# A two-layer hybrid decoder step on one core: opening with later slot requests, products of ones, and squares added pairwise

## The reference, cut to what matters

```python
def rmsnorm(x, gain):
    y = xf * lax.rsqrt(jnp.mean(xf * xf, axis=-1, keepdims=True) + RMS_EPS)
    return (y * gain.astype(jnp.float32)).astype(x.dtype)
...
def swiglu(x, w_gate, w_up, w_down):
    return (jax.nn.silu(x @ w_gate) * (x @ w_up)) @ w_down
...
    x = x + 0.5 * swiglu(rmsnorm(x, ffn1_norm), ffn1_w_gate, ffn1_w_up, ffn1_w_down)
```

## Time and profile before

| | us |
|---|---|
| median of 3 runs | 1161.32 (1161.1 to 1161.77) |
| profiled execution, its time | 1161.36 |
| its span, first to last instruction | 1159.3 |
| TensorE busy in the span | 1148.5 |
| GpSimd, VectorE, ScalarE busy | 806.0, 598.5, 532.8 |
| DMA | 180.91 MB, mean 156 GB/s |

### The profile page before, as it was taken

One profiled execution on the slowest core, in us unless ns is written; L12 is line 12 of the kernel. 1 busy time (PEld: TensorE's weight loads), 2 busy tenths in 40 slices (PEclk: granted clock), 3 DMA queues, 4 the chain that ended last, 5 costly groups with the idle time before them and its releaser, 6 DMA issues.

```text
span 1159.3 us, 22766 instructions
## 1 busy us (share of the span) xinstructions
PE 1148.5 (99%) x7914; PEld 1132.1 (98%) x7914; DVE 598.5 (52%) x878; ACT 532.8 (46%) x801; POOL 806.0 (70%) x421
## 2 busy tenths in 40 slices
PE   7999999999999999999999999999999999999999
PEld 6999999999899999999999999999998999999998
DVE  5865562239967544432258655522598764444100
ACT  5444444444765444444444444444457654444332
POOL 6776667777776766667667766677786776666674
DMA  8444445557535544445565444455573654443453
GB/s 295 153 162 146 145 118 149 149 171 221 159 120 165 173 146 154 143 122 148 159 196 161 147 146 146 119 149 162 179 211 114 183 154 153 152 152 124 138 149 107
DMA packets 72203, 180.91 MB, mean 156 GB/s; under 512 B 10210, under 2 KB 25826, under 8 KB 72162
## 3 DMA queue, kind: packets, MB, share of 16 engines
q1 hardware_dynamic: 71680, 179.23, 49.8%
q10 hardware_dynamic: 482, 1.16, 0.3%
HBM read 176.78 MB, written 3.58 MB: 156 GB/s over the span
## 4 chain that ended last, share of the span: by engine, by line
PE 96%; DMA 1%; DVE 1%; ACT 1%; POOL 0%; issue 0%; SPq 0%; DVEq 0%
PE bank L611 28%; PE bank L614 28%; PE bank L612 28%; PE bank L897 2%; PE bank L899 2%; PE bank L898 2%; PE bank L671 1%; PE bank L672 1%; PE bank L670 1%; DMA x<-in_xT 1%; DMA raw<-in_w 0%; PE bank L879 0%; PE bank L857 0%; PE bank L732 0%; PE bank L839 0%; POOL w_lo L506 0%
## 5 line engine op out<-in xcount | busy, mean ns | idle before, releaser
L506 POOL TENSOR_TENSOR w_lo<-raw,w_hi 128x1024 fp32r<-128x1024 f32 (+2 forms) x351 | 766.5, 2189 | 321.0 <-ACT w_hi L985 320.5
L985 ACT ACTIVATE w_hi<-raw 128x1024 fp32r<-128x1024 f32 (+2 forms) x351 | 336.5, 961 | 439.2 <-PE bank L614 423.2
L611 PE MATMUL bank<-xg_hi,w_hi 128*128 128x320 f32 x1552 | 481.8, 310 | 0.9 <-DVE tmp L1264 0.9
L614 PE MATMUL bank<-xg_hi,w_lo 128*128 128x320 f32 x1552 | 479.6, 309 | 0.0
L612 PE MATMUL bank<-xg_lo,w_hi 128*128 128x320 f32 x1552 | 479.5, 309 | 0.0
L611 PEld LDWEIGHTS bank<-xg_hi,w_hi 128*128 128x128 f32 x1552 | 291.3, 188 | 3.7 <-issue 1.9
L612 PEld LDWEIGHTS bank<-xg_lo,w_hi 128*128 128x128 f32 x1552 | 291.4, 188 | 0.4
L614 PEld LDWEIGHTS bank<-xg_hi,w_lo 128*128 128x128 f32 x1552 | 291.3, 188 | 0.0
L611 PE MATMUL bank<-h_hi,w_hi 128*128 128x320 f32 x704 | 217.5, 309 | 0.0
L612 PE MATMUL bank<-h_lo,w_hi 128*128 128x320 f32 x704 | 217.5, 309 | 0.0
L614 PE MATMUL bank<-h_hi,w_lo 128*128 128x320 f32 x704 | 217.5, 309 | 0.0
(11 more groups left out here) (188 smaller groups left out, 816.6 us busy)
## 6 DMA issues: line engine op xcount, KB each, us to landing
raw<-in_w SPq DMA_DIRECT2D x223, 512.0 KB, 3.8
raw<-in_w SPq DMA_DIRECT2D x64, 384.0 KB, 3.0
raw<-in_w SPq DMA_DIRECT2D x64, 320.0 KB, 2.9
k_all<-in_cache_kT SPq DMA_DIRECT2D x32, 128.0 KB, 3.5
v_past<-in_cache_v SPq DMA_DIRECT2D x32, 128.0 KB, 2.8
cst<-in_consts ACTq DMA_DIRECT2D x1, 997.0 KB
out_yT<-x SPq DMA_DIRECT2D x1, 960.0 KB, 4.9
x<-in_xT SPq DMA_DIRECT2D x2, 320.0 KB, 3.8
```

What stands on the lines that cost most here:

```text
L506: pool.tensor_tensor(w_lo[:, j, 0:count * P], raw[:, j, 0:count * P], w_hi[:, j, 0:count * P].bitcast(F32), ALU.subtract).then_inc(split.s ...
L611: pe.matmul(out, hi, in_hi[:, k, :], start=first and n == 0, stop=False)
L614: mm = pe.matmul(out, lo, in_hi[:, k, :], start=False, stop=last and end)
L985: act.activation(w_hi[:, j, 0:count * P], raw[:, j, 0:count * P], ACT.Copy).then_inc(split_hi.sem, 1)
```

## The change

Six edits, all in the opening of layer 0, and one in the order of layer 0's first step:

1. SyncE waits for piece 1 of the input before it requests slots (0,1) to (0,3). It then requests slot (1,0), ahead of `load_small`; the three other slots of iteration 1 follow behind it, and the loop starts at iteration 2.
2. The matrix of ones is filled first, with a semaphore of its own. TensorE multiplies ones with ones (128 columns, float32, into bank 7, never read) twelve times before its first real product, and once behind each of the eight high x high products of column 0.
3. The squares of tiles 0 to 3 move from ScalarE to VectorE, right behind the low parts of their piece. Tiles 4 and 5 are ScalarE's, behind its rounding of slot (0,1); 6 and 7 are VectorE's.
4. The `tensor_reduce` over eight squares becomes four additions: tiles 0, 1 + 2, 3; 4, 5 + 6, 7; the two results (640 elements each); and the last pair into `sumsq` (320). Each waits for the one before it.
5. TensorE's `sum_squares` stands behind column 1 instead of column 2.
6. In `first_step` of layer 0 the root comes before the rounding of slots (1,0) and (1,1), as in layer 1.

```diff
+WARM_PRODUCTS = 12
...
             load_x(2)
+            sp.wait_ge(x_in[1].sem, 16)
             for j in range(1, 4):
                 load_slot(0, BASE_G1, 0, j, w8, W8_G1, HALVES8)
+            load_slot(0, BASE_G1, 1, 0, w8, W8_G1 + 1, HALVES8)
             for L in range(DEPTH):
                 load_small(L)
-                with sp.Fori(1, IT_G) as i:
+                for j in range(0 if L else 1, 4):
+                    load_slot(L, BASE_G1, 1, j, w8, L * W8_ROWS + W8_G1 + 1, HALVES8)
+                with sp.Fori(2, IT_G) as i:
                     load(L, BASE_G1, i, w8, L * W8_ROWS + W8_G1 + i, HALVES8)
...
+            def idle_products(count):
+
+                for _ in range(count):
+                    pe.matmul(bank[7][:, 0:P], ones[:, :], ones[:, :], start=True, stop=True)
+
...
                     pe.matmul(bank[j][:, 0:TOK], w_hi[:, j, k * P:(k + 1) * P], xg_hi[:, k, :], start=k == 0, stop=False)
+                    if j == 0:
+                        idle_products(1)
...
                     if j == 0:
+                        pe.wait_ge(ones_ok.sem, 1)
+                        idle_products(WARM_PRODUCTS)
                         first_part(j, range(0, 4), half_hi.sem, 1, half_lo.sem, 1)
...
-                    if j == 2:
+                    if j == 1:
                         sum_squares(0, 0)
...
-                if L:
-                    root_of_norm(L, 0)
+                root_of_norm(L, 0)
                 round_slot(L, BASE_G1, 1, 0, HALVES8)
                 round_slot(L, BASE_G1, 1, 1, HALVES8)
-                if L == 0:
-                    root_of_norm(L, 0)
...
             round_first(1, raw_in[0].sem)
-            for d in range(DT // 2 - 2):
+            round_piece(2)
+            round_slot(0, BASE_G1, 0, 1, HALVES8)
+            for d in range(4, 6):
                 square_first(d)
-            round_piece(2)
-            for d in range(DT // 2 - 2, DT // 2):
-                square_first(d)
-            for j in range(1, 4):
+            for j in range(2, 4):
                 round_slot(0, BASE_G1, 0, j, HALVES8)
...
+            dve.memset(ones[:, :], 1.0).then_inc(ones_ok.sem, 1)
...
+            def squares_too(d):
+                dve.tensor_tensor(tmp[:, d, :], x[:, d, :], x[:, d, :], ALU.mult).then_inc(squared_too.sem, 1)
+
+            def add_squares(out, a, b, count):
+                dve.wait_ge(squared_too.sem, count)
+                return dve.tensor_tensor(out, a, b, ALU.add)
+
             for n, piece in enumerate(X_PIECES):
                 dve.wait_ge(x_in[n].sem, 16)
                 for d in range(*piece):
                     input_rest(d, d, d)
-            for d in range(DT // 2, DT):
-                dve.tensor_tensor(tmp[:, d, :], x[:, d, :], x[:, d, :], ALU.mult).then_inc(squared_too.sem, 1)
-            dve.wait_ge(squared_first.sem, DT // 2)
-            dve.wait_ge(squared_too.sem, DT // 2)
-            dve.tensor_reduce(sumsq[:, :], tmp[:, :, :].rearrange("p d t -> p t d"), AX.X, ALU.add).then_inc(summed.sem, DT)
+                for d in range(*piece) if n < 2 else range(6, 8):
+                    squares_too(d)
+            add_squares(tmp[:, 0:2, :], tmp[:, 0:2, :], tmp[:, 2:4, :], 6).then_inc(squared_too.sem, 1)
+            dve.wait_ge(squared_first.sem, 2)
+            add_squares(tmp[:, 4:6, :], tmp[:, 4:6, :], tmp[:, 6:8, :], 7).then_inc(squared_too.sem, 1)
+            add_squares(tmp[:, 0:2, :], tmp[:, 0:2, :], tmp[:, 4:6, :], 8).then_inc(squared_too.sem, 1)
+            add_squares(sumsq[:, :], tmp[:, 0, :], tmp[:, 1, :], 9).then_inc(summed.sem, DT)
```

More of the change, by code:

```diff
@@ L248, in hybrid_decoder @@
         filled = sig("filled", 0)
+        ones_ok = sig("ones_ok", 0)
         hist_ok = sig("hist_ok", 4)
@@ L1227, in _ @@
             dve.sem_inc(taken.sem, 4)
-            for n, (ap, value) in enumerate(((stat[:, 42:43], 1.0), (stat[:, 60:61], RMS_EPS), (stat[:, 61:62], LN_EPS), (ones[:, :], 1.0), (q_pad[:, :, :, :], 0.0),
+            dve.memset(ones[:, :], 1.0).then_inc(ones_ok.sem, 1)
+            for n, (ap, value) in enumerate(((stat[:, 42:43], 1.0), (stat[:, 60:61], RMS_EPS), (stat[:, 61:62], LN_EPS), (q_pad[:, :, :, :], 0.0),
                                              (conv_in[:, :, 0:CONV_HIST], 0.0), (pool_in[:, :, 0:POOL_HIST], 0.0))):
```

## The result

| | before | after |
|---|---|---|
| median of the runs, us (lowest to highest, number) | 1161.30 (1160.99 to 1162.02, 6) | 1166.59 (1166.50 to 1167.15, 6) |
| profiled execution, us | 1161.36 | 1166.54 |
| its span, us | 1159.3 | 1164.7 |
| first product of iteration 1, us | 27.02 | 32.60 |

The changed kernel is slower: ratio 1.0046, interval 1.0035 to 1.0056. It lies outside the 0.2% that such a measurement can tell from no change, 1.1 us above the forecast of 1165.5 and inside the range.

What follows compares the result with a forecast made beforehand. TensorE's products set the time after 27 us, so only the start of iteration 1 could move. A late sum of squares moved it 4.2 us: 1161.36 + 4.2 = 1165.6, forecast 1165.5, range 1159.5 to 1169.0.

Steps and rivals of the forecast that it cites:

- The term that decides: VectorE's squares and additions alternate with GpSimd's splits; sum of squares ready at 23.62 us, iteration 1 4.2 us later.
- the listing by hand: Step-by-step times for VectorE and GpSimd from 6.09 us: splits, squares, low parts, then four additions ending at 23.62.
- the sign: In the changed trace, VectorE squares taking 1.5 us and more, each ending 0.35 us after a split.
- The input and the slots: Opening loads: piece 1 landed at about 6.2 us, the input's last piece at 8.2, slot (0,1) at 10.8.
- the landing hardly matters: Slot (0,1) landing at 11.8 or 10.2 us would give the sum of squares at 23.2 or 23.5.
- The ones: TensorE's opening: twelve products take 5.1 us, 0.2 us late; eight in column 0 cost 1.7 to 3.4, hidden.
- The clock: TensorE's clock after standing 1 to 4.5 us before 23.7: no loss taken, 3.4 us kept as bound.
- The rival with this step: TensorE's clock falls in the new wait, adding 1.5 to 3.4 us: 1167.1 to 1169.0, chance 0.20.
- the forecast case: Late sum of squares in the opening without a clock fall: 1165.6 us, forecast 1165.5, chance 0.43.
- The sum: Whole kernel: profiled 1161.36 us plus 4.2 for iteration 1 starting at 31.24 instead of 27.02, 1165.6.
- keep its turn: VectorE goes first while instructions are lined up; sum of squares ready at 20.95, total near 1162.9, chance 0.20.
- the faster rival: VectorE's squares and additions run beside splits without waiting; sum by 15 us, 4.0 us gained, 1157.3, chance 0.15.

Runs made afterwards that it cites:

- e4: The kernel before, with only its tensor_reduce changed into four additions: 1166.39 us, ratio 1.0044.
- e1: The changed kernel with the one tensor_reduce in place of the four additions: 1160.85 us, ratio 0.9995 to the kernel before.
- e9: The kernel before, with its reduce replaced by seven additions onto a total in a PSUM bank, each with one SBUF input: 1161.11 us, ratio 0.9997.
- e3: The changed kernel with 26 more products of ones, never read, ahead of the sum of squares: 1165.27 us, ratio 1.0033 to the kernel before.
- e6: The changed kernel without SyncE's wait for input piece 1, so slots are requested at once: 1167.32 us, ratio 1.0051 to the kernel before.
- e8: The changed kernel without any products of ones: 1166.92 us, ratio 1.0049 to the kernel before.
- e2: The changed kernel with the sum of squares asked for behind column 2, as before: 1162.41 us, ratio 1.0008 to the kernel before.
- e11: The kernel of e10 without the products of ones: 1160.09 us, ratio 0.9988 to the kernel before.
- e5: The changed kernel with square 0 in a PSUM bank and seven additions onto it, each with one SBUF input: 1160.71 us, ratio 0.9994 to the kernel before.
- e10: The kernel of e5 with layer 0's small loads and the constants requested behind the slots of iteration 1: 1159.43 us, ratio 0.9983 to the kernel before.
- e12: The kernel of e7 with small loads and constants requested later, as in e10: 1162.82 us in two groups, ratio 1.0010 to the kernel before.
- e7: The kernel of e5 with each piece's squares added right behind it and slots requested at once: 1163.75 us in two groups, ratio 1.0022 to the kernel before.

## Why the prediction was right

The direction, the mechanism and, within 1.1 us, the size held. By its steps:

- **The term that decides** held in kind. The additions stood in line with the splits one by one, the sum was ready at 23.00 (forecast 23.62), and TensorE waited for it behind column 1. e4 shows that the additions alone do it, e1 that nothing is lost without them, e9 that it is the second SBUF input. Of the listing by hand, much did not happen in the profiled execution: the squares were not in line (0.44 us each, where one of 1.5 us or more was to be the sign), GpSimd stood from 10.61 to 14.45 with nothing to split, and the splits came after the squares rather than among them. The end agrees because three splits and the additions follow one another in either order: forecast, all splits, then all additions; measured, in turns. The nearness to 0.6 us is partly luck. That no square stood in line is a matter of that execution too: in the profiles of e3, e6 and e8, where VectorE runs the same squares, both pairs of tiles 0 to 3 took 1.96 to 1.98 us instead of 0.89, and in e1 and e2 one of them did, each behind a split of half of slot (0,0).
- **The input and the slots** were mis-sized. The last piece came at 10.05, not 8.2, and piece 1 at 6.92, not 6.2. Slot (0,1) came at 13.3, not 10.8, 1.5 later than before. I had divided the outstanding bytes by the full rate of the earlier trace rows; the runs do not show which part of that failed. Against the 10.53 of before, the input came 0.5 us sooner, not 2.3. The prediction said that the landing hardly matters, and e6 bears that out, with the slot rounded at 11.4 and no better time.
- **The ones** cost what was forecast (5.46 us against 5.1) and were hidden, not by a wait for VectorE, as forecast, but by slot (0,1), for which TensorE still stood 0.69 us behind column 0; e8 tells no difference. They did lift the clock early, which no wait let through to the end, and which is worth 0.66 us once the wait is gone (e11).
- **The clock** is the step that failed. I took nothing, arguing that the wait might be short, though my own listing had column 1 end at 19.2 and so a wait of 4.5. It was 4.69, and the fall cost 1.97 us in the profiled execution (9.54 us from the sum to iteration 1, against 7.57 in e3). The rival with this step, at 0.20, forecast 1167.1 to 1169.0: the measured 1166.59 lies between it and the forecast case, nearer to the rival, whose mechanism was there, towards the small end of its price.
- **The sum**: +4.22 forecast at iteration 1; 0.61 less by the earlier sum, 1.97 more by the clock, which is 5.58 measured: two errors of opposite sign, so that the total came nearer than the clock alone would have left it. Of this 5.4 us show in the span and 5.2 in the profiled execution; the last 0.2 lies outside the span, where it is 1.84 us after and 2.06 before, and 1.74 to 1.84 in the experiments, e4 and e9 among them. So 0.2 to 0.3 us of every difference to the kernel before is made outside the span, for a reason that no run shows; the 0.2 us of e9, and part of those of e1 and e5, are no more than that.
- **The other rivals** fell: VectorE did not keep its turn (2.7 us an addition), and the additions did wait. The squares ran at full speed in this execution, as the faster rival had it, but that alone gains nothing, and in e3, e6 and e8 they waited.

Why did such a rebuild gain nothing even without its additions (e1)? The reduce ends at 19.56, 0.2 us before that of the earlier trace rows, and TensorE now asks for it at 17.96. The column that ended sooner turned into a wait of 1.65 us. Only a sum that is earlier too (e5: 17.44) lets it through, and then slot (1,1) was late next, until e10.

## What to carry to other kernels

A long instruction that reads SBUF once can be better than several quick ones that read it twice, when GpSimd is busy beside VectorE: cost each of the quick ones as one whole GpSimd instruction, not by its own duration. Where a running sum is wanted, keep it in a free PSUM bank: seven additions then took 3.8 us, where four in SBUF took 11.3 and the reduce 4.9. And when a dependence is pulled forward in TensorE's order, add to the wait the price of the slow products behind it.

## What the runs showed of the hardware that was not expected

The clock fell after shorter waits than I had thought. From the sum of squares to iteration 1 there are 48 products in the changed kernel and 24 in e2 and e4; with e10, which did not stand, as the mark (7.65 us, or 4.12 with 24 products of 0.147 us less), the executions profiled read:

| | stood, us | sum to iteration 1, us | price, us |
|---|---|---|---|
| e1 | 1.65 | 7.69 | 0.0 |
| e2 | 2.20 | 5.69 | 1.6 |
| e4 | 3.47 | 5.74 | 1.6 |
| after | 4.69 | 9.54 | 1.9 |
| e8 | 4.69 | 9.04 | 1.4 |
| e6 | 5.62 | 10.07 | 2.4 |

The price follows the length of the wait only loosely (two waits of 4.69 us, 1.9 and 1.4); it was 1.4 to 2.4 us wherever the clock fell. Against e3 or e5 as the mark (7.57) it is 0.1 us more. In e12 the clock fell too, to 0.66 in 15 to 20 us, behind a wait of 2.15 in column 0. The Trainium skill ("TensorE: Matmul & The Clock Gate", Part 1) gives the slow state as the one to which an engine without work returns; the trace agrees, with granted clocks of 0.53 and 0.79 in the two stretches around the wait.

The rise of the clock at the start varies as well. Without the ones, four products still took 1.27 us from 13.72 in e11 and from 13.98 in e4, but 0.84 from 12.78 in e9 and 0.75 from 12.95 in e8.

Landings vary between executions and kernels with the same requests: slot (0,1) was rounded from 13.32 in the profile of after and from 11.31 in that of e2, whose first 18 us are the same program. The sum was ready at 23.00 and 22.61. The executions of e7 and e12 spread over 7 to 9 us, those of e10 over 0.8.
